# Gated heads: a level's queries and keys in one VectorE instruction over 2048 columns, none on GpSimd

## What is computed

```
b     = cumsum(logg, axis=3)                          # decay exponents of a chunk of 64 tokens
diff  = b[:, :, :, None, :] - b[:, :, None, :, :]
decay = where(mask3, exp(where(mask3, diff, 0)), 0)
att   = einsum('bhik,bhjk,bhijk->bhij', q, k, decay)
o     = einsum('bhik,bhkv->bhiv', q * exp(b), state) + einsum('bhij,bhjv->bhiv', att, v)
kdec  = k * exp(b_last - b)
state = exp(b_last) * state + einsum('bhjk,bhjv->bhkv', kdec, v)
```

## Time and profile before

| | us |
|---|---|
| median of 3 runs (lowest, highest) | 2231.57 (2223.7, 2233.25) |
| the profiled execution's own time | 2231.88 |
| its span, first to last instruction | 2230.2 |
| PE busy | 2075.2 (93%) |
| DVE busy | 1152.6 (52%) |
| ACT busy | 825.5 (37%) |
| POOL busy | 501.6 (22%) |

### The profile page before, as it was taken

How to read it: one execution, slowest core, us unless ns; L and a number is a source line. 1 busy time by engine, 2 the same in 40 slices (tenths; PEclk the granted TensorE clock), 3 DMA queues, 4 the chain that set the end, 5 groups by cost and what they waited for, 6 DMA issues and landing times. The chain is left out here.

```text
span 2230.2 us, 28839 instructions
## 1 busy us (share of the span) xinstructions
PE 2075.2 (93%) x10092; PEld 1688.7 (76%) x10092; DVE 1152.6 (52%) x2025; ACT 825.5 (37%) x1487; POOL 501.6 (22%) x375
## 2 busy tenths in 40 slices
PE   3799999999999999999997998999898986998998
PEld 3478888788878888887886786778787865886786
DVE  4546363555556463637344424677777684333423
ACT  3434343434334343425334212444434342333310
POOL 2123232232322232323200113123223231000010
PEclk7899999999999999999999998999999998999998
DMA  7222212212212212222414422210101012222512
GB/s 251 81 70 55 67 48 71 57 57 61 62 52 57 71 48 71 52 62 55 134 29 140 134 85 90 67 38 11 57 19 56 19 38 81 67 57 69 186 56 95
DMA packets 211553, 160.07 MB, mean 72 GB/s; under 512 B 8705, under 2 KB 196385, under 8 KB 210978
## 3 DMA queue, kind: packets, MB, share of 16 engines
q1 hardware_dynamic: 203762, 145.06, 21.7%
q0 software_dynamic: 4928, 8.70, 1.7%
q10 hardware_dynamic: 2800, 5.51, 0.7%
HBM read 130.56 MB, written 28.67 MB: 71 GB/s over the span
## 5 line engine op out<-in xcount | busy, mean ns | idle before, releaser
L283 DVE TENSOR_TENSOR w_lo<-w_raw,w_hi 128x512 fp32r<-128x512 f32 x303 | 268.2, 886 | 347.1 <-ACT w_hi L279 346.5
L207 PE MATMUL z_ps<-b_parts,w_hi 128*128 128x512 f32 x656 | 269.7, 411 | 20.4 <-ACT g_gate L217 12.3
L279 ACT ACTIVATE w_hi<-w_raw 128x512 fp32r<-128x512 f32 x308 | 192.7, 626 | 224.1 <-PE z_ps L312 100.9
L209 PE MATMUL z_ps<-b_parts,w_lo 128*128 128x512 f32 x656 | 263.3, 401 | 0.0
L310 PE MATMUL z_ps<-ah_hi,w_hi 128*128 128x512 f32 x608 | 247.2, 407 | 5.0 <-PEq L1887 4.3
L312 PE MATMUL z_ps<-ah_hi,w_lo 128*128 128x512 f32 x608 | 241.3, 397 | 0.0
L311 PE MATMUL z_ps<-ah_lo,w_hi 128*128 128x512 f32 x608 | 240.7, 396 | 0.0
L208 PE MATMUL z_ps<-b_parts,w_hi 128*128 128x512 f32 x560 | 226.1, 404 | 0.0
L192 DVE TENSOR_TENSOR w_lo<-w_raw,w_hi 128x1024 fp32r<-128x1024 f32 (+1 forms) x57 | 109.4, 1919 | 125.4 <-ACT w_hi L188 124.9
L207 PEld LDWEIGHTS z_ps<-b_parts,w_hi 128*128 128x128 f32 x656 | 127.3, 194 | 54.1 <-issue 25.9
L2114 POOL TENSOR_TENSOR g_E<-g_E,g_q 128x1024 f32<-128x1024 f32 x28 | 91.3, 3260 | 286.4 <-ACT g_E L2316 272.3
(11 more groups left out here) (403 smaller groups left out, 4213.8 us busy)
## 6 DMA issues: line engine op xcount, KB each, us to landing
w_raw<-in_a_win SPq DMA_DIRECT2D x220, 256.0 KB, 3.0
w_raw<-in_b_win SPq DMA_DIRECT2D x33, 512.0 KB, 4.1
y_scratch<-y SPq DMA_DIRECT2D x16, 512.0 KB, 3.0
w_raw<-in_a_wout SPq DMA_DIRECT2D x8, 768.0 KB, 5.8
w_raw<-in_b_wout SPq DMA_DIRECT2D x8, 768.0 KB, 6.1
xt_scratch<-work ACTq DMA_DIRECT2D x2, 2048.0 KB, 11.2
ares<-xt_scratch POOLq DMA_DIRECT2D x8, 512.0 KB, 3.9
y<-y_scratch SPq DMA_DIRECT2D x8, 512.0 KB, 4.5
```

Of the source, the lines that this page charges most:

```text
L207: pe.matmul(z_ps[s][:, 0:width], w_hi[slot][:, k, :], hi[k][:, tok], start=(k == 0), stop=False)
L209: mm = pe.matmul(z_ps[s][:, 0:width], w_lo[slot][:, k, :], hi[k][:, tok], start=False, stop=(k == nk - 1))
L279: act.activation(op_ring(w_hi, u), op_raw[i], ACT.Copy).then_inc(hi_op, 1)
L283: eng.tensor_tensor(op_ring(w_lo, u), op_raw[i], op_ring(w_hi, u).bitcast(F32), ALU.subtract).then_inc(lo_op, 1)
```

## The change

`q` and `k` become two halves of one tensor `qk`. DVE gets one function `operands` in place of `key_operands`, at the same places of its program; it multiplies both halves of an entry in one instruction over 2048 columns (entry 6: the query half alone, 1024 columns; entry 7: both halves times `k`, read twice). POOL's `operands` and the semaphore `opk_done` go. The waits of PE and ACT on `op_done` stay.

```diff
-            q, k = buf("q", [P, TOK]), buf("k", [P, TOK])
+            qk = buf("qk", [P, 2, TOK])
+            q, k = qk[:, 0, :], qk[:, 1, :]
@@ gpsimd
-                def operands(h, n):
-
-                    pool.wait_ge(e_done, NE * h + n + 1)
-                    if n == 0:
-                        for s in range(NS):
-                            pool.wait_ge(z_free[s], chunk(h, K) + 1)
-                    a = q if n < NL else k
-                    pool.tensor_tensor(E[n % 2][:, 0, :], E[n % 2][:, 0, :], a[:], ALU.mult).then_inc(op_done, 1)
...
-                        for e in entries(n):
-                            operands(h, e)
@@ tensor
                         pe.wait_ge(op_done, NE * h + i)
-                        if i < NL:
-                            pe.wait_ge(opk_done, (NE - 1) * h + i)
...
                     pe.wait_ge(op_done, NE * h + NE)
-                    pe.wait_ge(opk_done, (NE - 1) * (h + 1))
@@ vector
-                def key_operands(h, n):
-
-
+                def operands(h, n):
+
+
+                    dve.wait_ge(e_done, NE * h + n + 1)
+                    if n == 0:
+                        for s in range(NS):
+                            dve.wait_ge(z_free[s], chunk(h, K) + 1)
+                    e, x = E[n % 2][:], qk[:]
                     if n == NL - 1:
-                        return
-                    dve.wait_ge(e_done, NE * h + n + 1)
-                    dve.tensor_tensor(E[n % 2][:, 1, :], E[n % 2][:, 1, :], k[:], ALU.mult).then_inc(opk_done, 1)
+                        e, x = E[n % 2][:, 0, :], q
+                    if n == NL:
+                        x = k.rearrange("p (o t) -> p o t", o=1).to_broadcast([P, 2, TOK])
+                    dve.tensor_tensor(e, e, x, ALU.mult).then_inc(op_done, 1)
@@ rest, slot 0
                         pick(h, NL - 1)
-                        key_operands(h, NL)
+                        operands(h, NL)
                         pick(h, NL)
@@ head
                         for e in entries(n - 1):
                             if e < NL:
-                                key_operands(h, e)
+                                operands(h, e)
```

More of the change, by code:

```diff
@@ L2045, in stage @@
              dec_done, sub_done, e_done, op_done, qsub_done, qe_done, qi_done, zero_done, lev_done, mask_done, kd_ready,
-             opk_done, st_mm, st_done, vtr_done, v_ready, out_done, out_moved, sq_done, ssq_done, sd_done, rln_done, t_done,
+             st_mm, st_done, vtr_done, v_ready, out_done, out_moved, sq_done, ssq_done, sd_done, rln_done, t_done,
              y_done) = (sem("gla_" + n) for n in (
@@ L2049, in stage @@
                  "g_done", "scan_done", "dcol_done", "dec_done", "sub_done", "e_done", "op_done", "qsub_done",
-                 "qe_done", "qi_done", "zero_done", "lev_done", "mask_done", "kd_ready", "opk_done", "st_mm", "st_done",
+                 "qe_done", "qi_done", "zero_done", "lev_done", "mask_done", "kd_ready", "st_mm", "st_done",
                  "vtr_done", "v_ready", "out_done", "out_moved", "sq_done", "ssq_done", "sd_done", "rln_done",
```

## The result

| | before, us | changed, us |
|---|---|---|
| median of 5 runs (lowest, highest) | 2232.04 (2223.7, 2233.25, and one run of 8242.07, which counts in the median alone) | 2218.05 (2213.46, 2220.56) |
| ratio, 95% interval | | 0.994 (0.992 to 0.996) |
| the profiled execution | 2231.88 | 2220.56 |
| its span | 2230.2 | 2218.9 |

The forecast was 2218 (2211 to 2228). Timed once more, the same kernel gave 2211.32 against 2232.55, ratio 0.991 (0.988 to 0.994): two timings of one kernel lie 7 us apart in their medians, and their intervals overlap. The page's busy shares say little: PE and DVE are almost as before, POOL lost 100 us.

What follows compares the result with a forecast made beforehand. PE was taken to bound the kernel, waiting in the gated heads on a chain of DVE and ACT. Waits of 10.0 us plus 3.5 us of clock gave 13.5 us off 2231.88: 2218 us, range 2211 to 2228.

Steps and rivals of the forecast that it cites:

- What bounds, and the chain: PE bounds; in heads 1 to 3 DVE, then ACT's silu, then PE form a chain, worth up to 3.62 us.
- The stall, 2.0 and 2.2 us: DVE's instructions behind key halves stand still beside POOL's query half: 2.0 us at L2526's pair, 2.2 at L192.
- 2048 columns at 2.25 us: DVE's merged instruction per entry should cost 2.25 us, 1.10 more than the key half; bounds 2.2 and 2.46.
- Gate waits of about 0.3 and 1.6: PE's waits before L207 for ACT's silu: near 0.3 us in head 0, 1.6 in the others.
- Turning waits near 1.7, last 3.9: PE's waits before the keys are turned: near 1.7 us, 3.9 in the last head, full clock behind them.
- The cover of entry 6: Entry 6's 1.14 us on DVE hides in at least 1.23 us idle before L2440, heads 1 to 3.
- Sum of the waits, 10.0: PE's waits saved: 6.3 in heads 1 to 3, 2.2 head 0, 0.4 keys, 1.1 last head: 10.0 us.
- The clock, 3.5 taken, at most 5.3 and 1.5: PE's low clock behind 3.62 us waits should go: 3.5 us taken, bounds 0 and 5.3, 1.5 possible at head 0's turning.
- The total: Whole kernel: 13.5 us less, so 2218 us.
- The slower rival: POOL's help worth more than its harm, the stretch having another cause: 9.9 us slower, 2242 us; chance 0.05.
- The clock rival: PE's waits shrink but its clock doesn't recover: 2222 us; chance 0.28.

Runs made afterwards that it cites:

- the delays: Changed kernel, with one or two unused multiplications of 512 columns added on DVE ahead of entry 4's exponents: 2220.23 us and 2222.45 us.
- late_only: Kernel before, with DVE's merged multiplication for entries 2 and 3 alone, GpSimd keeping its query halves of the other six: 2226.03 us, ratio 0.996.
- the two shadow kernels: Changed kernel, with unused GpSimd work at each entry's exponential: a 1024-column multiplication (2243.5 us), or a one-column multiplication and three memsets (2214.58 us).
- the memset kernel: Changed kernel, with GpSimd running a one-column multiplication and three unused memsets of 1024 columns at each entry's exponential: 2214.58 us, ratio 0.992.
- shadow_read: Changed kernel, with GpSimd multiplying a constant SBUF tile by itself, 1024 columns, unused, at each entry's exponential: 2243.5 us, ratio 1.004.
- the early silu: Changed kernel, ACT making the first gate chunk's first silu in slot 8, before entry 4's exponential: 2215.76 us; together with the keys first: 2201.22 us.
- the keys first: Changed kernel, DVE making the last picks and entry 7's operands ahead of the next weight chunk's rounding, heads 1 to 3: 2209.85 us, ratio 0.988.

## Why the prediction was right, and where only its total was

- *What bounds, and the chain* (DVE from entry 2's exponents, ACT's silu, PE): right. Shown by the delays, 0.6 for 0.6, and by late_only, which removed the gate waits alone.
- *The stall, 2.0 and 2.2 us:* right in size, and its cause, only argued in the prediction, is now shown by the two shadow kernels.
- *2048 columns at 2.25 us:* 2.21.
- *Gate waits of about 0.3 and 1.6:* 0.33 and 1.74. DVE's part was as reckoned (entry 4's exponential 20.70 us behind the start of entry 2's exponents, 20.76 forecast); the rest is PE's: it began its last level before the wait 0.3 us sooner (20.99 us behind that start, 21.28 before the change), so it waited that much longer.
- *Turning waits near 1.7, last 3.9:* 1.68 three times, 3.90. The cover of entry 6 was thinner than in the trace of before, 0.36 us of idle time left in front of L2427, and held. That the clock stays full behind these waits came true in heads 0 to 2 and not behind the last one.
- *Sum of the waits, 10.0:* 9.5 and 9.6 measured. At the gates 5.6 in heads 1 to 3 for 6.3, and 1.1 in head 0; at the keys 1.1, 0.5 and 1.1, as reckoned.
- *The clock, 3.5 taken, at most 5.3 and 1.5:* the term of the sum that was mis-sized. 7.8 and 9.3 us measured in the stage. The gate waits of 3.62 lost their low stretches, all three, and beside them others shrank, such as behind the turned keys, where turning `t_ps` took 1.09 us in heads 0 to 2 of the changed kernel and 1.6 to 1.8 in the second profile of before. I had counted those out because they could move. One reading was too short as well: "behind 1.92 none" looked at head 1 alone, while in head 2 of the same profile turning `t_ps`, 1.3 us behind the same wait, took 1.97 us (it begins at 1722.22). Only the part at the gates, three low stretches in both profiles of before and in none of the changed kernel, is tied to a wait by the delays. The rest isn't: the memset kernel, with the same waits, took another 6 to 7 us off, so of the 7.8 and 9.3 some may be chance.
- *The total:* 13.5 forecast; 14.0 by the medians of the first timing, 21 by the second. That the first met the forecast to 0.1 us is partly luck: more clock won in the stage (7.8 for 3.5), and time lost outside it. Ahead of it that was scatter. Behind it, 2.9 and 1.4 us in the two pairs, a part is the low level, which now falls on the last head's state matmuls: the first four take 2.07 us in the changed kernel, 1.13 before. Whether the whole of it is that stays open.

The slower rival (POOL's help worth more than its harm) is refuted by shadow_read: it needed a stretch with another cause. The clock rival didn't come true: the gate waits left, 1.74, lie among those behind which the clock stayed full.

## What to carry to other kernels

A helper engine's instruction isn't free because it runs beside: look at the duration of the neighbour that runs with it. Here GpSimd's 2.40 us saved VectorE 1.1 us and cost it 2.1. When a wait is taken away, look for the next one that the same queue decides, and reckon how much slack it had; here 0.36 us let 5.5 us of removed waits bring 2.1 alone (PE's idle time in the stage 15.5 before, 13.4 with the early silu), and 4.2 once the queue behind it had been put in order (with the keys first: 12.2 without the early silu, 8.0 with it). And the matmuls' time isn't fixed by the waits: before a gain of a few us is credited to the clock, look at what it does in other runs with the same waits.

## What the runs showed of the hardware that I hadn't expected

A GpSimd multiplication of one column took 2.30 us, all but 0.2 of it waiting for VectorE's instruction of 2.29 us (with none beside it, the same one took 0.19). A multiplication of 1024 columns on GpSimd took 2.40 us with two different inputs and 1.90 with the same 512 columns, read twice over, as both. The PE clock fell about 1 us after PE had started again behind a wait of 2.33 us, not in the wait itself. Two profiles of one kernel agreed in the gate and turning waits to 0.02 us and differed in where the clock was low.
